# First layer's attention: the order of its rounds, their lags, and the low part as a step of its own

## The reference, cut to what matters

```
q, k, v = x @ w_in                       # 16 heads x 64, 512 positions
c = cumsum(log_sigmoid(f_logit + b_f))   # one gate row per head
for each block of 128 queries:
    logits = (q_block @ k.T) / 8 + c_query - c_key, masked causally
    p = softmax(logits)
    o = p @ v
h = o @ w_out;  x = layer_norm(alpha * x + h)
```

## Time and profile before

| | us |
|---|---|
| median of 3 runs | 2318.71 |
| lowest, highest | 2317.28, 2320.51 |
| the profiled execution | 2320.3 |
| its span | 2318.5 |
| TensorE busy in the span | 2186.9 (94%) |
| DVE, ACT, POOL busy | 1154.2 (50%), 1002.3 (43%), 941.9 (41%) |
| mean granted clock | 0.964 |

### The profile page before, as it was taken

One profiled execution on the slowest core, in us unless ns is written; L12 is line 12 of the kernel. 1 busy time (PEld: TensorE's weight loads), 2 busy tenths in 40 slices (PEclk: granted clock), 3 DMA queues, 4 the chain that ended last, 5 costly groups with the idle time before them and its releaser, 6 DMA issues.

```text
span 2318.5 us, 27955 instructions
## 1 busy us (share of the span) xinstructions
PE 2186.9 (94%) x10720; PEld 1817.2 (78%) x10720; DVE 1154.2 (50%) x1852; ACT 1002.3 (43%) x2027; POOL 941.9 (41%) x714
## 2 busy tenths in 40 slices
PE   7999899999998898799999999899999999999997
PEld 6788778888877777678888878677677887888886
DVE  3545565554343666465554354666664335444322
ACT  5656444443225555244443245655543234333222
POOL 3655553343356663353343442222412343322232
PEclk9999999999999999899999997999999999999998
DMA  4111123223222221122222211111112231222221
GB/s 159 55 55 58 53 91 109 91 91 102 100 71 81 92 74 46 37 73 101 100 91 102 100 62 66 37 37 37 37 46 91 100 109 55 109 91 93 100 100 53
DMA packets 29844, 183.06 MB, mean 79 GB/s; under 512 B 3984, under 2 KB 4112, under 8 KB 11920
## 3 DMA queue, kind: packets, MB, share of 16 engines
q1 hardware_dynamic: 29712, 181.27, 22.7%
HBM read 174.97 MB, written 2.10 MB: 76 GB/s over the span
## 4 chain that ended last, share of the span: by engine, by line
PE 83%; DVE 6%; ACT 5%; issue 3%; POOL 2%; DMA 0%; SPq 0%; POOLq 0%; DVEq 0%; ACTq 0%
PE PS L1454 81%; PE PS L1579 1%; POOL LO L2743 1%; DVE bQS L2194 1%; PE PS L1692 1%; ACT HI L1778 0%; DVE aQS L2194 0%; ACT cEM L2153 0%; DVE T_f L2266 0%; DVE XL L2271 0%; DVE YH L2296 0%; PE PS L1627 0%; POOL bTQ L2801 0%; ACT bP L1994 0%; DVE LO L2194 0%
## 5 line engine op out<-in xcount | busy, mean ns | idle before, releaser
L2743 POOL TENSOR_TENSOR LO<-RAW,HI 128x512 fp32r<-128x512 f32 (+2 forms) x382 | 541.3, 1433 | 627.0 <-ACT HI L1778 626.9
L1454 PE MATMUL PS<-XH,HI 128*128 128x512 f32 (+1 forms) x1584 | 638.0, 403 | 23.9 <-DVE XL L2194 7.0
L1454 PE MATMUL PS<-XH,LO 128*128 128x512 f32 (+1 forms) x1584 | 625.2, 395 | 0.0
L1454 PE MATMUL PS<-XL,HI 128*128 128x512 f32 (+1 forms) x1584 | 619.2, 395 | 2.2 <-DVE XL L2271 2.1
L1778 ACT ACTIVATE HI<-RAW 128x512 fp32r<-128x512 f32 (+3 forms) x668 | 366.2, 608 | 171.3 <-PE PS L1454 168.0
L2194 DVE TENSOR_TENSOR LO<-RAW,HI 128x512 fp32r<-128x512 f32 (+2 forms) x286 | 305.2, 1071 | 247.2 <-ACT HI L1778 246.8
L1454 PEld LDWEIGHTS PS<-XH,HI 128*128 128x128 f32 (+1 forms) x1584 | 302.3, 191 | 86.8 <-issue 21.5
L1454 PEld LDWEIGHTS PS<-XH,LO 128*128 128x128 f32 (+1 forms) x1584 | 301.4, 190 | 66.0 <-issue 1.1
L1454 PEld LDWEIGHTS PS<-XL,HI 128*128 128x128 f32 (+1 forms) x1584 | 301.6, 191 | 64.4 <-DVE XL L2271 3.6
L1454 PE MATMUL PS<-HH,HI 128*128 128x512 f32 x528 | 205.4, 389 | 0.0
L1454 PE MATMUL PS<-HL,HI 128*128 128x512 f32 x528 | 205.4, 389 | 0.0
(11 more groups left out here) (404 smaller groups left out, 3326.6 us busy)
## 6 DMA issues: line engine op xcount, KB each, us to landing
RAW<-wall SPq DMA_DIRECT2D x138, 1024.0 KB, 4.8
RAW<-wall SPq DMA_DIRECT2D x24, 896.0 KB, 4.5
bROT<-bTQ SPq DMA_DIRECT2D x64, 64.0 KB, 2.0
RAW<-wall SPq DMA_DIRECT2D x5, 512.0 KB, 3.2
XF<-xT SPq DMA_DIRECT2D x4, 512.0 KB, 5.5
outT<-XR SPq DMA_DIRECT2D x8, 256.0 KB, 2.0
FP<-cfp SPq DMA_DIRECT2D x1, 1024.0 KB, 6.7
MKF<-cmask SPq DMA_DIRECT2D x1, 704.0 KB, 11.0
```

The lines of the kernel that those rows point to most:

```text
L1454: return e.matmul(out, a, b, start=start, stop=stop)
L2743: return e.tensor_tensor(out, x, h.bitcast(F32), ALU.subtract)
```

## The change

`LAGF` with its six lags goes. The stage `sc` is split: the scores stay `sc`, DVE's maxima become a step `smx`. The stage `ft` is split: ACT's high part stays `ft`, DVE's low part becomes `fd`. A round now has two parts with a yield after each: the first puts values (lag 8), high part (4), low part (4), scores (0) and transpose (3); the second puts maxima (0), exponential (0) and reciprocal with scaling (1). Before, the lags were: transpose 4, scores with maxima 0, exponential 1, reciprocal and scaling 2, high and low part 5, values 10, in the order values, parts, scaling, exponential, scores, transpose. The two rates that advance this generator are doubled, 0.37 to 0.74 and 0.9 to 1.8. The waits name the new steps.

```
--- before.py
+++ after.py
@@ -137,12 +137,11 @@
 
 
 
-LAGF = (4, 0, 1, 2, 5, 10)
 STATES = ((0, 0, 0), (1, 0, 0), (0, 0, 1), (0, 1, 0), (1, 1, 0), (1, 0, 1), (0, 2, 0), (1, 2, 0), (0, 1, 1), (1, 1, 1), None,
           (0, 2, 1), (1, 2, 1))
 LAGS = (0, 1, 2, 3, 4, 6)
 LAGD = (4, 0, 1, 2, 3, 5, 10)
-RATES = (0.37, 0.18, 1.12, 1.4, 1.0, 0.9, 0.9)
+RATES = (0.74, 0.18, 1.12, 1.4, 1.0, 1.8, 0.9)
 AHEAD = 5
 HEADS = (0, 4, 1, 5, 2, 6, 3, 7)
 ROPED = (0, 4, 1, 2, 3)
@@ -162,11 +161,13 @@
     "qeq": (("qh", 1), ("ql", 1)),
     "qek": (("kh", 1), ("kl", 1)),
     "nb": (("nb", 1), ("nbc", 1)),
-    "sc": (("qk", 1), ("mx", 1)),
+    "sc": (("qk", 1),),
+    "smx": (("mx", 1),),
     "ex": (("exp", 1),),
     "dg": (("rec", 1), ("dg", 1)),
     "fl": (("flip", 1),),
-    "ft": (("pth", 1), ("ptl", 1)),
+    "ft": (("pth", 1),),
+    "fd": (("ptl", 1),),
     "tu": (("turn", 1), ("oh", 1), ("ol", 1)),
     "res": (("res", 1),),
     "statm": (("sma", 1), ("smu", 1)),
@@ -344,6 +345,16 @@
         yield
 
 
+def parted(items, parts):
+
+    for n in range(len(items) + max(lag for part in parts for _, lag in part)):
+        for part in parts:
+            for stage, lag in part:
+                if 0 <= n - lag < len(items):
+                    yield from stage(items[n - lag])
+            yield
+
+
 def unit_sequence():
     out = [("f", 0), ("aqk", 0), ("av", 0), ("aqk", 1), ("aqk", 2), ("av", 1), ("aqk", 3), ("aqk", 4), ("av", 2),
            ("aqk", 5), ("aqk", 6), ("av", 3), ("aqk", 7)]
@@ -660,7 +671,7 @@
                 gate_row(0)
             s = put("sc", h, i)
             at_bank(s, 2 + (4 * h + i) % 2)
-            freed[2 + (4 * h + i) % 2] = ("mx", s)
+            freed[2 + (4 * h + i) % 2] = ("mx", ("smx", h, i))
             sent[0] = 4 * h + i + 1
             if i == 2 and h < 15:
                 gate_row(h + 1)
@@ -671,6 +682,10 @@
             at_bank(s, b)
             freed[b] = ("nbc", s)
 
+        def maxima(it):
+            put("smx", *it)
+            yield from ()
+
         def power(it):
             put("ex", *it)
             yield from ()
@@ -684,7 +699,11 @@
             yield from ()
 
         def taken(it):
-            freed[ag.bank_of[("fl",) + it]] = ("ptl", put("ft", *it))
+            put("ft", *it)
+            yield from ()
+
+        def rest(it):
+            freed[ag.bank_of[("fl",) + it]] = ("ptl", put("fd", *it))
             yield from ()
 
         def values(it):
@@ -709,7 +728,9 @@
         chores.append(gates(t))
         put("cst")
         vunit(0)
-        alongside(rounds([(h, i) for h in range(16) for i in range(4)], [flip, scores, power, diag, taken, values], LAGF), RATES[0])
+        alongside(parted([(h, i) for h in range(16) for i in range(4)],
+                         [[(values, 8), (taken, 4), (rest, 4), (scores, 0), (flip, 3)],
+                          [(maxima, 0), (power, 0), (diag, 1)]]), RATES[0])
         for kind, i in [("q", 1), ("q", 2), ("v", 1), ("q", 3), ("q", 4), ("v", 2), ("q", 5), ("q", 6), ("v", 3), ("q", 7)]:
             if kind == "q":
                 if i >= 2:
@@ -1439,7 +1460,7 @@
                 rotate(ag.order[i - 3][1])
             load_raw(i)
             if ag.order[i] == ("up0", 4):
-                e.wait_ge(*when("mx", "sc", 15, 3))
+                e.wait_ge(*when("mx", "smx", 15, 3))
                 e.wait_ge(*when("flip", "fl", 15, 3))
                 e.dma_start(FP[:, 1152:3200], cfp[:, 1152:3200]).then_inc(s_tab, 16)
         for j in range(8):
@@ -1581,7 +1602,7 @@
             elif kind == "va":
                 h, kb = a
                 if kb == 0:
-                    e.wait_ge(*when("ptl", "ft", h, 3))
+                    e.wait_ge(*when("ptl", "fd", h, 3))
                     if h % 4 == 0:
                         e.wait_ge(*when("vl", *whole["avs", h // 4, 3]))
                 v = 1024 * (h // 4 % 2) + 256 * kb + 128 * (h // 2 % 2)
@@ -1912,12 +1933,12 @@
                 h, = a
                 e.wait_ge(*when("nb", *step))
                 if h > 1:
-                    e.wait_ge(*when("mx", "sc", h - 2, 3))
+                    e.wait_ge(*when("mx", "smx", h - 2, 3))
                 act(blk(aNB, h % 2), PS[bank][:, :], ACT.Copy).then_inc(SEM["nbc"], 1)
             elif kind == "ex":
                 h, i = a
                 n, kl = 4 * h + i, 128 * (i + 1)
-                e.wait_ge(*when("mx", "sc", h, i))
+                e.wait_ge(*when("mx", "smx", h, i))
                 p = blk(aP, n % 4)[:, 0:kl]
                 act(p, p, ACT.Exp, bias=aNM[:, n:n + 1], accum_out=aSU[:, n:n + 1]).then_inc(SEM["exp"], 1)
             elif kind == "ft":
@@ -2380,11 +2401,11 @@
                     r, c = slice(64 * x, 64 * x + 64), u + 512 * x
                     m = diff(aQS[64 - 64 * x:128 - 64 * x, c:c + 512], PS[ag.tiles[t].bank][r, :], aQS[r, c:c + 512])
                 m.then_inc(SEM["kl"], 1)
-            elif kind == "sc":
+            elif kind == "smx":
                 h, i = a
-                n, kl = 4 * h + i, 128 * (i + 1)
+                n, kl, bank = 4 * h + i, 128 * (i + 1), ag.bank_of["sc", h, i]
                 mx, nm = aMX[:, n:n + 1], aNM[:, n:n + 1]
-                e.wait_ge(*when("qk", *step))
+                e.wait_ge(*when("qk", "sc", h, i))
                 if i == 0:
                     e.wait_ge(*when("nbc", "nb", h))
                 if n > 3:
@@ -2399,11 +2420,11 @@
                 n = 4 * h + i
                 e.wait_ge(*when("exp", "ex", h, i))
                 e.reciprocal(aRC[:, n:n + 1], aSU[:, n:n + 1]).then_inc(SEM["rec"], 1)
-            elif kind == "ft":
+            elif kind == "fd":
                 h, i = a
                 p = 1664 * (h % 2) + 128 * i
                 h_, l_ = (aPX[:, z + p:z + p + 384 * (i + 1)].rearrange("p (k n) -> p k n", n=384)[:, :, 0:128] for z in (0, 3328))
-                e.wait_ge(*when("pth", *step))
+                e.wait_ge(*when("pth", "ft", h, i))
                 diff(l_, PS[ag.bank_of["fl", h, i]][:, 0:128 * (i + 1)].rearrange("p (k n) -> p k n", n=128), h_).then_inc(SEM["ptl"], 1)
             elif kind == "va" and a[1] == 3:
                 h, kb = a
```

1 line of the change is left out of this document (removed).

## The result

| | us | ratio to before, 95% interval |
|---|---|---|
| before, median of 4 (2317.28 to 2320.51) | 2318.57 | |
| changed, median of 4 (2352.3 to 2360.6) | 2357.77 | 1.0164 [1.0148, 1.0179] |
| forecast | 2348 (2316 to 2360) | |
| profiled executions, before and changed | 2320.3 and 2357.09 | |

Slower, by 39 us where 30 were forecast. The profiled executions differ by 36.8 us, and all but 2.0 of them arise before the eighth step of the first output-projection tile, the one that waits for the last two heads.

A forecast was written before the change was run, and what follows sets the result against it. TensorE bounds the kernel, so only its waits or slower clock count. Stalls of 37.2 less 15.5 give 21.7, clock 7.8, sum 29.5; 2320.3 + 29.5 - 1.6 = 2348 us, range 2316 to 2360.

The forecast's parts named there:

- start: At step 16, item 3's transpose waits behind a key tile's copies and subtractions: 4.2 us, then 0.7 at head 0's values.
- heads 1, 4, 8: First values of these heads wait for the low part behind a query tile, maxima and exponential: 3.2, 3.4, 3.2 us.
- heads 5, 9, 12: First values of these heads wait behind a query tile, maxima and exponential out of the chain: 2.1, 2.4, 1.8 us.
- gate rows by a key tile: Gate-row rounds at steps 34, 82, 129 meet a key tile and wait 1.3, 1.1, 1.3 us.
- first scores: First scores behind a finished query/key unit, the second one step behind instead of two: about 4.2 us, before 3.6.
- unit end, heads 13, 14, 15, last: Tail: last unit's end 2.8 stays, heads 13, 14, 15 wait 0.7, 1.4, 2.0, the last 1.4 stays; sum 8.3 us.
- clock, more than before: Stalls clearly over 2.12 us slow TensorE's clock: five new dips of 1.7 us, less 0.7 at head 0: 7.8 us.
- DVE's freed time worth nothing: DVE's maxima no longer wait for a transpose; DVE is off the path, so priced 0, bounds 0 and 15.5 us.
- The chain of head 1: After a query tile: mx(10), ex(10), aOH, pth, ptl in series from DVE free at 78.56 to 82.1; wait 3.2 us.
- faster: Rival: freed DVE has low parts always there first; gate-row, half the start and 2.1 tail waits go: 2311 us, chance 0.13.
- Half price: Rival: the chains overlap more than summed, collisions cost 11 us without more clock dips: 2330 us, chance 0.17.
- The rival taken from the weight-load share: Rival: TensorE is held back inside its busy time, the new order releases up to 46 us: 2273 at most, chance 2%.

## Why the prediction was right

The direction, the mechanism and most places came out; it was short by 10 us, in the terms that follow.

| step | forecast | trace |
|---|---|---|
| start | 4.2, and 0.7 at head 0 | 4.26, none; and 0.87, 0.67, 0.40 before it |
| heads 1, 4, 8 | 3.2, 3.4, 3.2 | 2.93, 3.14, 3.10 |
| heads 5, 9, 12 | 2.1, 2.4, 1.8 | 2.01, 2.25, 1.99 |
| gate rows by a key tile | 1.3, 1.1, 1.3 | 1.30, 1.14, 1.74 |
| first scores | 4.2 together | 2.10, 2.10 |
| unit end, heads 13, 14, 15, last | 2.8, 0.7, 1.4, 2.0, 1.4 | 2.75, 0.25, 1.91, 2.08, 1.41; and 0.73 at a gate row |
| all waits | 37.2 | 39.2 |
| clock, more than before | 7.8 | 10.2 in the stretch |

- *Nothing added on TensorE:* right by the program. Its matmul busy time grew by 6.5 us, which I put down to matmuls at half clock; no run shows it apart.
- *DVE's freed time worth nothing:* right. Its 40.6 us of waits for transposes ahead of the maxima are gone from the list; ACT's waits for the maxima rose from 18.3 to 79.9 us, the price of exponentials straight behind them, and DVE's waits for ACT's high part from 6.2 to 42.8.
- *The chain of head 1:* forecast link by link from the earlier trace rows and found link by link: 3.5 us from DVE being free to the first values, and 3.5 in the trace (85.37 to 88.88). The start's sum took 2.75 us for a key tile where the earlier trace rows give 2.62, which changes nothing that counts.
- *The clock:* the mis-sized term, 7.8 us for a measured 10.2. I let only waits clearly over 2.12 us bring the low clock, so 5 more stretches, and there are 6. Four of the five came (start, heads 1, 4, 8). The fifth did not: the 2.25 at 220.43 had none. The trace has one at 230 us behind a wait of 1.74 instead, and another from 301 us behind the wait of 2.08 at 300.35. That the number of stretches came out so close is in part luck, as the rule behind it failed. The 0.7 taken off for a wait at head 0 fell away with that wait. This term and the small waits at the start make 4.4 us of what was missed; 2.0 lie behind the attention, 0.9 is unexplained, and the medians differ by 2.4 more than the profiled pair. So the last aOH matmul came 36 us later (before at 303.81, now at 340.19), where the signs named 25 to 30.
- *Rivals:* faster is out, since the gate-row waits it would have removed rose from 3.0 to 4.9 us. Half price is out, as six heads wait 15.4 us in all where 16.1 were forecast at full price. The rival taken from the weight-load share needed the time to fall, and it rose. The page it names (Trainium skill, "Perfetto Trace Analysis", Identifying the Most-Contended Engine) takes that share as a measure of TensorE's headroom; whether there is headroom inside the busy time no run here shows.

The runs added what the forecast did not have: its two reasons, the shorter distance and the longer chain, each cost 21 to 27 us alone, and easing either by itself gives back only 10 to 12, while easing both gives 30.

## What to carry to other kernels

Before shortening a lag in a schedule with in-order queues, list for each consumer what stands ahead of its producer in both engines' queues when the rarest long step (here a tile's evacuation, 2.6 to 3.8 us) falls in between, and compare with the bottleneck's work in that gap. Here a chain that crosses two engines inside half a round wanted longer lags, not shorter. And after removing one wait look for the backlog it had hidden: judge by the sum of the bottleneck's waits, not by the wait aimed at.

## What was not expected of the hardware

TensorE's time at half clock came behind its waits, but the length of one wait near 2 us does not tell whether it comes. In the kernel before, the clock stayed full behind the wait of 2.08 us at 63.81 (the window that the earlier trace rows show, 62 to 64, holds the wait itself; the one behind it is below). In the kernel whose heads open later, the same matmul waits the same 2.08 us at 65.27, and the clock falls (first row the kernel before, second row this one; the clock is the third number from the right):

```profile
64.00:66.00 2.00, 1.57 (x11) 1.01 (x11) 1.28 (x7) 1.46 (x4) 2.00 (x2) 1.00 0.00 0
...
66.00:68.00 2.00, 1.81 (x7) 1.29 (x8) 0.93 (x6) 1.41 (x4) 1.52 (x2) 0.50 0.00 0
```

In the changed kernel it stayed full after 2.25 us and fell after 1.74. So which wait brings a stretch could not be forecast from its length, and each stretch costs 1.7 us. In the seven kernels with 9 us or more of new waits, a microsecond of new waits cost 1.4 to 1.7 us of time (39 us for 23.7 in the changed one, 26 for 14.9 with the exponential moved), and the share beyond the wait itself was mostly the clock. In the kernels with fewer new waits the clock can cost more than the waits do.
